# Two side tasks change their place in a hand-woven schedule: the gates' chain starts later beside RWKV, RGLRU's constant moves beside GDN

## The reference, cut to what matters

```python
def first_block(x, ...):
    n = rmsnorm(x, attn_norm[l])
    u = n @ w_in[l]
    y_gdn = gated_deltanet(u_gdn, ...)       # g = -exp(a_log) * softplus(a_raw + dt_bias), cumsum by chunk
    y_mlstm = mlstm(u_mlstm, ...)            # log_f = log_sigmoid(f_raw + b_f), running maxima
    y_rglru = rglru_block(u_rglru, ...)      # log_a = -8 * r * softplus(-lambda)
    y_rwkv = rwkv7_time_mix(u_rwkv, ...)
    x = x + mix @ w_out[l]
    ...
```

## Time and profile before

| | |
|---|---|
| median of 3 runs | 2398.09 us (2397.85 to 2399.14) |
| the profiled execution, its own time | 2399.12 us |
| its span, first to last instruction | 2397.3 us |
| mean granted PE clock over the span | 0.998 |
| PE busy | 2372.0 us, 99% |
| DVE busy | 1464.2 us, 61% |
| ACT busy | 1129.7 us, 47% |

### The profile page before, as it was taken

How to read it: one execution, slowest core, us unless ns; L and a number is a source line. 1 busy time by engine, 2 the same in 40 slices (tenths; PEclk the granted TensorE clock), 3 DMA queues, 4 the chain that set the end, 5 groups by cost and what they waited for, 6 DMA issues and landing times.

```text
span 2397.3 us, 31305 instructions
## 1 busy us (share of the span) xinstructions
PE 2372.0 (99%) x12920; PEld 1972.0 (82%) x12920; DVE 1464.2 (61%) x1891; ACT 1129.7 (47%) x1423; POOL 97.0 (4%) x79
## 2 busy tenths in 40 slices
PE   9999999999999999999999999999999999999998
PEld 7777789888888888888888888888888888888887
DVE  6887657787745555555555666555555655555555
ACT  6635446554544344444444464455434455444444
POOL 1000011210000000000000130000000000000000
PEclk9999999999999999999999999999999999999999
DMA  9644355655655555555555575555445544555563
GB/s 303 196 135 126 109 171 198 209 181 179 219 190 179 193 192 181 189 187 197 183 189 187 182 251 188 193 176 174 160 163 188 189 146 150 200 191 190 191 237 141
DMA packets 245613, 443.48 MB, mean 185 GB/s; under 512 B 7392, under 2 KB 72544, under 8 KB 243168
## 3 DMA queue, kind: packets, MB, share of 16 engines
q1 hardware_dynamic: 241984, 423.65, 53.5%
q0 software_dynamic: 2912, 17.30, 2.0%
q10 hardware_dynamic: 576, 0.53, 0.1%
HBM read 430.97 MB, written 10.49 MB: 184 GB/s over the span
## 4 chain that ended last, share of the span: by engine, by line
PE 92%; DVE 4%; ACT 1%; issue 1%; DMA 0%; POOL 0%; SPq 0%; ACTq 0%; POOLq 0%; DVEq 0%
PE pp L664 25%; PE pp L666 25%; PE pp L665 25%; PE pp L693 7%; PE pp L694 3%; PE ps L623 2%; DVE ringL L1977 1%; PE ps L1276 1%; PE ps L1290 1%; PE ps L812 0%; DMA raw<-in_w_in 0%; ACT ringH L1364 0%; DVE AR L2524 0%; PE pp L699 0%; PE pp L700 0%
## 5 line engine op out<-in xcount | busy, mean ns | idle before, releaser
L1977 DVE TENSOR_TENSOR ringL<-raw,ringH 128x1024 fp32r<-128x1024 f32 x779 | 963.5, 1243 | 681.0 <-ACT ringH L1364 679.2
L1364 ACT CAST ringH<-raw 128x1024 fp32r<-128x1024 f32 x779 | 814.4, 1049 | 973.9 <-PE pp L666 863.2
L664 PE MATMUL pp<-ringH,nS 128*128 128x512 f32 x1376 | 543.9, 395 | 0.0
L666 PE MATMUL pp<-ringH,nS 128*128 128x512 f32 x1376 | 536.4, 390 | 0.0
L665 PE MATMUL pp<-ringL,nS 128*128 128x512 f32 x1376 | 535.9, 389 | 0.0
L693 PE MATMUL pp<-nS,ringH 128*128 128x512 f32 x992 | 363.4, 407 | 6.1 <-DVE ringL L1971 2.3
L666 PEld LDWEIGHTS pp<-ringH,nS 128*128 128x128 f32 x1376 | 258.3, 188 | 54.4
L664 PEld LDWEIGHTS pp<-ringH,nS 128*128 128x128 f32 x1376 | 258.5, 188 | 52.5 <-issue 0.4
L665 PEld LDWEIGHTS pp<-ringL,nS 128*128 128x128 f32 x1376 | 258.6, 188 | 51.3 <-issue 0.2
L694 PE MATMUL pp<-nS,ringL 128*128 128x256 f32 x992 | 279.3, 282 | 0.0
L664 PE MATMUL pp<-ringH,xS 128*128 128x512 f32 x704 | 277.2, 394 | 0.0
(11 more groups left out here) (400 smaller groups left out, 1922.1 us busy)
## 6 DMA issues: line engine op xcount, KB each, us to landing
raw<-in_w_in SPq DMA_DIRECT2D x189, 1024.0 KB, 5.1
raw<-in_ffn_w_gate SPq DMA_DIRECT2D x44, 1024.0 KB, 5.1
raw<-in_ffn_w_up SPq DMA_DIRECT2D x44, 1024.0 KB, 5.1
raw<-in_ffn_w_down SPq DMA_DIRECT2D x44, 1024.0 KB, 5.0
raw<-in_w_out SPq DMA_DIRECT2D x32, 1024.0 KB, 5.0
raw<-in_w_mem_kv SPq DMA_DIRECT2D x16, 1024.0 KB, 5.6
raw<-in_w_proj_a SPq DMA_DIRECT2D x8, 1024.0 KB, 5.1
raw<-in_w_proj_m SPq DMA_DIRECT2D x8, 1024.0 KB, 5.0
```

What stands on the lines that cost most here:

```text
L664: mm(o, XH[:, ts(j)], WH, first, False)
L666: t_of[0] = mm(o, XL[:, ts(j)], WH, False, last)
L1364: e.copy(ringH[:, h % NSPL, 0:nh * cols], raw[:, u % NRAW, h0 * cols:(h0 + nh) * cols]).then_inc(*hi.tick(h))
L1977: tt2(ringL[:, h % NSPL, o], raw[:, u % NRAW, h0 * cols:(h0 + nh) * cols], ringH[:, h % NSPL, o].bitcast(F32), SUB).then_inc(*lo.tick(h))
```

## The change

Three edits. First, `beside_rwkv` advances `scan` only at the first three halts of `mem`; after `mem` the rest of `scan` (pieces 5 to 14) runs one piece at each of RWKV's halts 1 to 10. Second, `lambda` leaves that place and opens `small_mixers`, the side of GDN: its first three pieces at GDN's first halt, one more at each of the next four. Third, POOL's two memsets of padding columns move from the stage `lambda` to the stage `scan`, at its piece 12.

```diff
 def small_mixers(L):
+    constant = L.stage("lambda")
+    next(constant)
+    next(constant)
+    for _ in constant:
+        yield
     while not L.done("r1") and "gdn" not in L.open:
         yield
...
     scan = L.stage("scan")
     next(scan)
     yield
-    for _ in L.stage("mem"):
-        next(scan, None)
+    for n, _ in enumerate(L.stage("mem")):
+        if n < 3:
+            next(scan)
         yield
     yield from scan
-    yield from L.stage("lambda")
     while not L.done("m0"):
         yield
...
-            def lam(L):
-                for _ in range(6):
+            def scan(L):
+                for _ in range(11):
                     yield
                 e.wait_ge(*nx_p.at("r"))
                 for g in range(4):
...
-            course(lane(unit, {"begin": begin, "lambda": lam, ...
+            course(lane(unit, {"begin": begin, "scan": scan, ...
```

More of the change, by code:

```diff
@@ L3036, in xc @@
                 yield
-            course(lane(unit, {"begin": begin, "lambda": lam, "square": square, "gdn": gdn, "rglru": rglru, "gains": gains, "xf": finals, **{f"split2.{q}": split2(q) for q in range(4)}, "mk": mk, "mv": mv, "xc": xc}))
+            course(lane(unit, {"begin": begin, "scan": scan, "square": square, "gdn": gdn, "rglru": rglru, "gains": gains, "xf": finals, **{f"split2.{q}": split2(q) for q in range(4)}, "mk": mk, "mv": mv, "xc": xc}))
         def sync(e, S, ring, lane):
```

## The result

The changed kernel takes 2402.43 us in the median of 20 runs (2400.84 to 2405.12), the one before 2399.12 us (20 runs, 2397.64 to 2402.07). The ratio is 1.0013, with a 95% interval of 1.0007 to 1.0019: slower by 3.3 us. The interval excludes a ratio of 1, but all of it lies inside the 0.2% that the prediction called no measurable change. The profiled execution of the changed kernel took 2403.80 us, its span is 2401.9, 4.6 over that of before. Every line number behind the first edit is five higher than before (the cut is now L1982, `rk`'s matmul L950).

What follows compares the result with a forecast made beforehand. PE, busy 99% of the span, was taken to bound the kernel; -1.5 + 2.25 - 0.5 + 3.55 = +3.8 us on 2398.1 gave 2401.9 us, range 2395.5 to 2406.0.

Steps and rivals of the forecast that it cites:

- Part 1: Nine calls before RWKV: both PE waits for DVE's cut go, -1.5 us, bounds 0 and -1.5.
- Part 2: RWKV's halts 1 to 10: +2.25 us, bounds +0.15 and +3.5; then -0.5 as PE's wait in the inversion goes.
- The start: RWKV's start: DVE waits for the memory's third quarter before its shifts; PE waits about 2 us near 73 us.
- The Ln: RWKV's halt 3: DVE idles 0.6 us for ACT's Ln; 1.9 us if Tanh needs its own table load.
- `rk`: RWKV's halt 8: row 0.5 us earlier, PE's wait 2.1 us in place of 1.3, next weights 0.75 us later.
- Part 3: GDN's first five halts: the constant's pieces delay the convolutions' cuts, +3.55 us, bounds 0 and 5.7.
- pieces 4 and 6: Constant's pieces in GDN's convolutions: 0.8 us each added, of which 0.3 us each is idle time now.
- Lower bound: GDN's convolutions: 0 us lost, if the casts turn out to be paced by PE.
- the rival of a hidden constant: GDN's convolutions: PE has more in hand, nothing lost there; 2398.4 us, or 2396.3 with lower Part 2; chance 0.22.
- The drain: GDN's wait for Exp: the skill's drain of about 1380 ns would add 1.38 us, sum +5.2; the trace lacks it.
- The clock's rival: RWKV's new waits of 2.0 and 2.1 us make PE's clock fall, 3.4 us lost; 2405.3 us, chance 0.20.
- The bounds 2399.5 and 2404.5: Whole kernel: the forecast time's own bounds in us, said to be those of the two large terms.

Runs made afterwards that it cites:

- cuts_ahead: gates_alone with DVE's four shifts one halt later, behind the gates' piece 5 and two cuts, the wait for the memory's third quarter left in place; 2401.40 us.
- gates_alone: The changed kernel, but the constant's seven pieces run beside GDN only after its convolutions, from about 415 us; 2399.80 us.
- constant_late: The kernel before, gates unmoved, with the constant beside GDN after the convolutions and POOL's memsets as in the change; 2397.79 us.
- col_ahead: The changed kernel, but PE's twelve matmuls of the gates' piece 12 run one halt earlier, ahead of PE's wait for rk; 2402.59 us.
- exp_ahead: The changed kernel, but the constant's Abs and Exp run on ACT right behind the gates' last Exp; 2400.45 us.
- constant_alone: The kernel before with only the constant's move to GDN's first five halts and POOL's memsets, the gates as before; 2400.80 us.
- both_tuned: Constant after the convolutions, two cuts ahead of DVE's first shift and its memory wait, DVE's gates' piece 7 in call 9, later pieces one or two halts later; 2400.27 us.
- constant_spread: The changed kernel, but the constant's pieces run one a halt over GDN's first seven halts; 2409.51 us.
- landing_covered: gates_alone with DVE's four shifts one halt later and the wait for the memory's third write moved directly before the first shift; 2397.14 us.

## Why the prediction held

**Part 1, -1.5.** Measured -1.53. One of the two waits stayed, 0.33 us at 61.11, but cut and matmul had both come 0.35 us earlier; the other went.

**Part 2, +2.25, then -0.5.** Measured +2.4 and -0.6. The start: first shift at 71.55, released by the DMA (by the prediction 0.4 us before 71.82), PE's wait 2.20 us (about 2), near 73. cuts_ahead shows its cause. The Ln: L2156 at 80.60 behind 0.68 us (0.6, at about 80), and Tanh (L1590) without a table load. `rk`: L950 at 101.15 (101.2), next weights 0.83 later (0.75). The idle time at the inversion (L859 now) is gone, as expected. The sum of this part holds two effects that gates_alone and constant_late take apart: the gates' move costs about 1.5 us, with part 1's gain counted in, and the constant's leaving gives 1.6 back. One step was wrong: PE was to arrive there 1.3 us earlier and wait 2.1. It arrived 0.5 earlier and waited 1.29, because piece 10's four matmuls (89.47 to 90.43) had moved in front of that wait too, and I had only counted them as gone from their old place. Since `rk` sets the start, the sum did not notice. That piece 12's matmuls are what makes the next weights late is by the order of rows; col_ahead was to show it alone and the clock spoiled it.

**Part 3, +3.55.** Measured +3.23. The cut behind the first halt is 2.71 us late (2.67), PE waits 1.20 + 1.15 + 0.30. The delay is carried from halt to halt and not caught up, as I said. Over-sized were pieces 4 and 6: exp_ahead, where they stand with 0.52 from the first halt, has 1.02 in all, so they cost 0.5 together and not 1.0. Lower bound and the rival of a hidden constant are refuted by constant_alone.

**The drain.** By the Trainium skill (ScalarE: Activation LUTs, "What ACT_TABLE_LOAD costs") each switch of table sets would cost some 1.4 us more than its load. Here the load of 373.27 ends at 374.55 and Exp starts at 374.56, and ahead of the load ACT is busy up to 373.25; the trace disagrees, as in the earlier trace rows.

**Sum and rivals.** +3.8 predicted, +3.5 in the traces without the clock, +3.3 between the medians. The clock's rival happened in part: no fall between 70 and 110 us behind the new 2.2 and 1.3 us, but in cuts_ahead behind 2.50 us and in both_tuned behind 1.81. So it was right to price it, but the length of the wait alone does not tell. The prediction also read the earlier trace rows too kindly: of the 2.7 us of waiting between 150 and 170, at full clock there, one single wait is 2.23 us, hardly shorter than the longest beside mLSTM (2.29), behind which the clock fell. The bounds 2399.5 and 2404.5 around the forecast follow from no sum that it shows: with part 2's own bounds alone it would be 2399.8 and 2403.2, with part 3's alone 2398.4 and 2404.1. That the time came out within 0.5 us is in part luck: the median from which the prediction counted was 1.0 too low (2398.09, and 2399.12 over 20 runs), and the change 0.5 too large (3.8, and 3.3).

## What to carry over

When an edit frees time on one engine, look for the next event that does not move with it (a landing transfer, a row that another engine computes) and ask which of the freed work can run ahead of that wait; here the wait behind two cuts and a gates' piece won 1.8 us in the traces. But ask first whether the edit that made the work wait there is worth it: the schedule that left the gates alone was as fast. A small table-driven function at the head of a dependent chain costs its load and its latency; here they were 2.2 us, the 28 operations behind it 1.0. In a woven schedule a halt is a resource like any engine: before a side task is spread over more of them, count who stands behind it, transfers too.

## What the runs showed of the hardware

The granted clock varies between executions of one kernel. In its trace the kernel before lost about 3 us to it near 256 us; in constant_late's, with the same waits of 3.6 us in all at L1109, it did not fall there, but near 158. PE waits 2.2 us for L862 in all twelve traces; the clock fell behind it in eight of them, and not in before, constant_alone, constant_spread and col_ahead. Runs of the whole change at a mean clock of 0.995 took 2404.6 us on average (4 runs), those at 0.996 2403.2 (5), at 0.997 2401.8 (8) and at 0.998 2402.1 (3).

It also falls where PE has no idle time at all. In constant_late PE is busy 20.00 of 20 us and the clock is 0.91:

```profile
400.00:420.00 20.00, 20.00 (x202) 19.71 (x201) 15.31 (x22) 13.67 (x18) 2.87 (x4) 0.91 0.73 252
```

Shortly before it fell PE ran this:

```profile
407.84 2.03 PE L893 MATMUL ps<-cm,AR 128*64 128x1 f32 x64
```

These are 64 matmuls of one column, some 3 us ahead of the fall, without idle time. The same 64 stand at 411.7 in the kernel before, where the clock stays at 1.00 from 400 to 430. Why it falls in one execution and not in the other, no run here shows.

DVE and POOL stood in each other's way. In landing_covered this is POOL's timeline:

```profile
67.57 1.80 POOL L2919 TENSOR_TENSOR AR<-AR 128x512 f32<-128x512 f32 x1 [7.88 <-DVE AR L1991]
```

DVE's piece 5 starts at 68.23 beside it, takes 1.30 us and ends at 69.53, just behind POOL's end at 69.37; where POOL is idle the same operation takes 0.41. The Trainium skill (SBUF — State Buffer, "Who interferes with whom") says that such an operation and POOL's share a pair of ports, which the first to start holds to its end; the trace agrees in so far as DVE's operation takes 0.89 us longer and ends behind POOL's. That it ends only 0.16 us behind, less than its own 0.41, stays open; times on POOL are rough. In the kernel before, the cut that starts at 52.68, just behind POOL's operations from 52.46, takes 2.05 us where the next ones take 1.21.
